# A transformer backbone in float32 halves on one core: three reorderings of the Vector engine's work, and wider pieces on GpSimd

## The chip, the cores and the metric

One core of one Trainium2 chip runs the whole program. The metric is the device time in microseconds (us) of one execution. The engines are TensorE (PE in the profile; PEld is its weight load), the Vector engine (DVE), the Scalar engine (ACT), GpSimd (POOL) and SyncE (SP), which issues the loads. "The profile" and "the trace" are one execution recorded by the hardware profiler.

## What is computed

Two layers over 512 latent tokens (`xl`) and 256 context tokens (`xc`) of width 1024. Each has a mixer (Fourier groups with neighbourhood attention, then differential attention) and a squared-ReLU MLP. DEPTH is 2, and layer 0 does the same for the context. The parts that the change touches, cut from the reference:

```python
def modulate(x, g, shift, scale):
    return rms_norm(x, g) * (1.0 + scale) + shift

def squared_relu_mlp(h, w_in, w_out):
    return jnp.square(jax.nn.relu(h @ w_in)) @ w_out

for i in range(DEPTH):
    ml = jnp.split((c_act @ w_mod[i] + b_mod[i])[:, None, :], 6, axis=-1)
    ...
    xl = xl + ml[5] * squared_relu_mlp(modulate(xl, norm_mlp_g[i], ml[3], ml[4]), w_mlp_in[i], w_mlp_out[i])
    ...
```

## The kernel before

**Numbers in two halves.** Each float32 operand is split in a high part (`w_hi`, `h_hi`, `hidh`) and a low part (`w_lo`, `h_lo`, `hidl`), and TensorE makes three products of the halves (lines 2090 to 2092, in `three`). Weights come in units of 128x1024. SyncE loads a unit into `raw` (four slots), the Scalar engine writes `w_hi` (`high_u`, `high_b`, `high_sum`), and GpSimd subtracts for `w_lo` (`low`, line 744), in as many pieces as its argument says; `lo_made` counts finished units. TensorE's `unit_done` frees the slot of `w_hi`, and `lo_made` the slot of `raw`.

**Every engine works through its own list in order.** The lists are written out by hand, and semaphores tie them together. So an instruction that waits holds up everything behind it on its engine.

**The first MLP** (`first_mlp` on each engine) has eight blocks of 512 hidden columns for 768 tokens. Block 0 is computed directly: the Scalar engine takes the relu of four tiles into `hidl_f`, the Vector engine squares each in place (`first_square`, line 1701), the Scalar engine rounds it into `hidh`, and the Vector engine makes `hidl` (`first_low`, line 1705). TensorE's `second(0, ...)` multiplies them with W_out: output tile 0 asks for `hq_made` (the four `hidl`) one after the other, and output tile 2 asks that tile 0 has been added to x by the Vector engine (`add_tile(0, 0)`, line 1662, counted by `x_added`). Blocks 1 to 7 use a seven-product scheme: GpSimd makes sums of the quadrants a11, a21, a12, a22 of the weights (`summed`, line 770), and the Vector engine makes the matching operands t1 to t4 of the activations once, in `difference` and `less` (lines 1689 to 1697): three instructions of 128x1536 for t1, and seven for t3, t2 and t4. `turn_high` and `turn_low` split them. The eighth block (`b == 7`) follows the sixth without a second product between them; I call that the last border. There GpSimd's `outer_sums` come behind `low(w, 4)`.

**The modulation vectors.** `mod_step(c, k)` on the Vector engine adds one of eight rows of chunk c (lines 1438 and 1441) from `mod_ring`, a ring of four buffers. Its last step also makes `acc_hi` and `acc_lo` (lines 1450, 1451). TensorE spreads the sum (`mod_mm`, lines 2131 and 2132), and `extract_late` takes the result out. SyncE's `load_mod` waits until the ring's buffer has been used, and all loads queued behind it wait too.

**The second MLP** (`mlp`) has four blocks of 16 units for 512 tokens, 24 matmuls of 512 columns a unit. Units 0 to 7 of a block give the hidden tiles (`hidden`, lines 1672, 1675, 1676, three Vector instructions), units 8 to 15 add to x. In its first block the Vector engine also does chunks 10 and 11. Before, chunk 10 stands at units 0 to 3, and `mod_mm(10, 6)` behind unit 5; chunk 11 stands at units 6, 7 and 8, and `mod_mm(11, 6)` behind unit 10. `MOD_LATE` says behind which unit's load SyncE issues which rows. The Scalar engine makes `w_hi` three units ahead, then the relu of the unit (line 1143), and its relu into one of two buffers waits for the Vector engine's first instruction of two tiles before. GpSimd's pieces are 1024 columns wide here, before and after.

Of the kernel before, what the change touches and what calls it, by code (L numbers as in the profile page):

```python
# [21 lines left out]
ALU = mybir.AluOpType  # L22
# [33 lines left out]

BLOCKS = 8
MOD_OF = {1: [0], 2: [1], 3: [2], 4: [3], 5: [4, 5], 6: [6], 7: [7]}
MOD_LATE = {1: (10, (4, 5)), 2: (10, (6, 7)), 4: (11, (0, 1)), 5: (11, (2, 3)), 7: (11, (4, 5)), 8: (11, (6, 7))}
M0, M1 = FIRST["mlp0"], FIRST["k1"]  # L60
RAWS = 64

# [5 lines left out]
def block_raw(b):  # L68
    return 8 * b if b < 7 else 52
# [60 lines left out]
def build(nc, t):  # L130

    ctx = ExitStack()
    with ctx:
# [602 lines left out]
        def _(pool):  # L736
            def low(u, pieces=1, b=None):

                pool.wait_ge(hi_made, u + 1 if b is None else u + 1 + 16 * b)
                r, s = raw_of(u), u % SLOTS  # L740
                src = w_sum if r is None else raw[:, r % SLOTS]
                for p in range(pieces):
                    sl = slice(p * (1024 // pieces), (p + 1) * (1024 // pieces))
                    ins = nc.gpsimd.tensor_tensor(w_lo[:, s, sl], src[:, sl], w_hi[:, s, sl].bitcast(F32),  # L744
                                                  op=ALU.subtract)
                ins.then_inc(lo_made, 1)
# [18 lines left out]
            def first_mlp():  # L765

                def summed(dst, a, b, op):
                    for p in range(4):
                        sl = slice(256 * p, 256 * p + 256)
                        ins = nc.gpsimd.tensor_tensor(dst[:, sl], a[:, sl], b[:, sl], op=op)  # L770
                    ins.then_inc(w_sums, 1)

                for w in range(4, 8):
                    low(M0 + w, 4)
                for b in range(1, BLOCKS):
                    w, r, n = M0 + block_first(b), M0 + block_raw(b), 4 * (b - 1)
                    a11, a21, a12, a22 = (raw[:, (r + j) % SLOTS] for j in range(4))

                    def raw_here(j):
                        pool.wait_ge(raw_in[(r + j) % SLOTS], 16 * ((r + j) // SLOTS + 1))  # L780

                    def outer_sums():
                        raw_here(1)
                        raw_here(3)
                        if b == 1:
                            pool.wait_ge(t_lo, 2)
                        else:
                            pool.wait_ge(lo_made, M0 + block_first(b - 1) + 4)
                        summed(w_sum, a21, a22, ALU.add)
                        raw_here(0)  # L790
                        pool.wait_ge(w_sums, n + 1)
                        summed(a21, a11, a21, ALU.subtract)

                    if b < 7:
                        outer_sums()
                    low(w, 4)
                    if b == 7:
                        outer_sums()
                    pool.wait_ge(w_sums, n + 2)
                    pool.wait_ge(lo_made, w + 1)  # L800
                    summed(a11, w_sum, a11, ALU.subtract)
                    low(w + 1, 4)
                    raw_here(2)
                    pool.wait_ge(w_sums, n + 3)
                    pool.wait_ge(lo_made, w + 2)
                    summed(w_sum, a12, a11, ALU.subtract)
                    for j in range(2, 11 if b < 6 else 7):
                        low(w + j, 4)
                for w in range(8):
                    low(M0 + LAST_W + w, 4)  # L810
                for u in range(AHEAD):
                    low(M1 + u, 4)

            def mlp():
                u0 = FIRST["mlp1"] + AHEAD + 1
# [610 lines left out]
        def _(dve):  # L1426
# [252 lines left out]
            def first_mlp():  # L1679
# [23 lines left out]
                def first_low(i):  # L1703
                    dve.wait_ge(hq_hi, i + 1)
                    tt(hidl[:, i], hidl_f[:, i], hidh[:, i].bitcast(F32), op=ALU.subtract).then_inc(hq_made, 1)  # L1705
# [3 lines left out]
                first_square(0)  # L1709
                first_square(1)  # L1710
                first_square(2)
                first_low(0)
                dve.wait_ge(tf_made, 1)
                difference(t3f[:], t4f[:], 1, H1, 0, H1)
                first_low(1)
                first_low(2)
                first_square(3)
                less(t2f[:], t1f[:], 1, 1, H1)
                first_low(3)
                less(t4f[:], t2f[:], 3, 1, H0)  # L1720

                def add_tile(b, m):
                    w = M0 + block_first(b) + (7 if b else 4) + m // 2
# [21 lines left out]
                for b in range(1, BLOCKS):  # L1745
                    c = MOD_OF[b][0]

                    def joined(side, p, q):
                        dve.wait_ge(unit_done, M0 + block_first(b) + p + 1)
                        dve.wait_ge(s_copied, 3 * (b - 1) + (3, 2, 1)[q])  # L1750
                        if q < 2 and b < 7:
                            dve.wait_ge(x_added, xa(0, min(b, 6) - 1, 7) + 1)
                        elif q < 2:
                            dve.wait_ge(hq_made, 4 * b)
                        tt(quarter_ps(b, q), part_ps(b, side), quarter(b, q)[2], op=ALU.add).then_inc(s_added, 1)

                    def low(q):
                        hi, lo, _ = quarter(b, q)
                        dve.wait_ge(hq_hi, 4 * b + q + 1)
                        tt(lo, quarter_ps(b, q), hi.bitcast(F32), op=ALU.subtract).then_inc(hq_made, 1)  # L1760

                    early = 4 if b < 5 else 6
                    steps(c, range(early))
                    joined(1, 3, 0)
                    steps(c, range(early, early + 1))
                    low(0)
                    joined(0, 4, 1)
                    steps(c, range(early + 1, early + 2))
                    low(1)
                    if b == 6:  # L1770
                        extract_late(c, 4)
                    joined(1, 5, 2)
                    low(2)
                    low(3)
                    if b < 5:
                        for m in range(8):
                            add_tile(b, m)
                            if m < 2:
                                steps(c, range(6 + m, 7 + m))
                            if m == 4:  # L1780
                                extract_late(c, 0)
                    elif b == 5:
                        add_tile(b, 0)
                        add_tile(b, 1)
                        extract_late(c, 0)
                        for m in range(2, 6):
                            steps(c + 1, range(2 * m - 4, 2 * m - 2))
                            add_tile(b, m)
                        add_tile(b, 6)
                        extract_late(c + 1, 0)  # L1790
                        add_tile(b, 7)
# [14 lines left out]
            def mlp():  # L1806
                u0 = FIRST["mlp1"]

                def blk(b, first, last):
                    for i in range(12 if last else 16):  # L1810
                        u = u0 + i
                        if i < 8:
                            hidden(b, i)
                        else:
                            if first and i in (8, 12):
                                dve.wait_ge(mod_done, PE_MODS + i // 4 + 9)
                            add_x(1, u + 16 * b + 1, u % 2, i - 8, 5, xa(1, b, i - 8))
                            if last and i > 8:
                                sum_squares(4, i - 9)
                        if first:  # L1820
                            if i == 5:
                                extract_late(10, 6)
                            elif i == 10:
                                extract_late(11, 6)
                            for k in (range(2 * i, 2 * i + 2) if i < 4 else {6: (0, 1, 2), 7: (3, 4, 5), 8: (6, 7)}.get(i, ())):
                                mod_step(10 if i < 4 else 11, k)

                blk(0, True, False)
                with st.loop(1, HID_BLOCKS - 1, 8) as b:
                    blk(b, False, False)  # L1830
                blk(HID_BLOCKS - 1, False, True)
# [253 lines left out]
        def _(pe):  # L2085
# [269 lines left out]
            def mlp(layer=1):  # L2355
# [3 lines left out]
                def blk(b, first, last):  # L2359
                    for i in range(12 if last else 16):  # L2360
# [21 lines left out]
                        elif i >= 8:  # L2382
                            unit(u + 16 * b, u % SLOTS, u % 2, *hid_t, chunks,
                                 (lambda k: pe.wait_ge(hid_made, ha(layer, b, k) + 1)) if i == 8 else None)
                        if first and i in (5, 10):
                            mod_mm(10 if i == 5 else 11, 6)

                blk(0, True, False)
                with pe.Fori(1, HID_BLOCKS - 1) as b:
# [571 lines left out]
```

## Time and profile before

| | us |
|---|---|
| median of 3 runs (1621.24 to 1622.34) | 1621.82 |
| the profiled execution: its time | 1622.5 |
| its span, first to last instruction | 1620.7 |
| TensorE busy in the span | 1578.3 (97%) |
| Vector / Scalar / GpSimd busy | 960.7 / 605.1 / 824.6 |

The profiled execution's time is 1.8 us more than its span, which lies around it. Times in the rows are us from the start of the span, an instruction's own duration in the lists of groups is in ns. A releaser after an arrow is what ended the idle time before an instruction.

### The profile page before, as it was taken

The page shows a single profiled execution, that of the slowest core. Times are in us where ns is not written, and L with a number is a line of the kernel's source. Part 1 is how long each engine was busy: PE and PEld are TensorE (multiplying, and loading weights), DVE is VectorE, ACT ScalarE, POOL GpSimd, SP SyncE. Part 2 cuts the span into 40 slices and gives each one's busy share as a digit, 9 for nine tenths or more (in the row PEclk, how much of TensorE's full clock was granted, in tenths as well). Part 3 has the DMA queues.
Part 4 walks back from the last instruction along what each step waited for, and adds up shares of the span by engine and source line. Part 5 has one row for each costly group of instructions (what it writes and reads, how often), then busy time and mean ns, then how long its engine had stood idle before and what let it go on. Part 6 is the DMA issues. An engine that isn't in the chain of part 4 may idle for free.

```text
span 1620.7 us, 23732 instructions
## 1 busy us (share of the span) xinstructions
PE 1578.3 (97%) x9272; PEld 1411.6 (87%) x9272; DVE 960.7 (59%) x1362; ACT 605.1 (37%) x1009; POOL 824.6 (51%) x778
## 2 busy tenths in 40 slices
PE   8999999997999999999899999999999799999998
PEld 5889988987999999999898888878889678888887
DVE  4697457258655555647466778059956755344264
ACT  4422466334243352441542411258844222222222
POOL 2422465337867868768852634245325444444441
PEclk9999999998999999999999999999999899999999
DMA  8473212212142242243352323110012342322221
GB/s 347 193 268 148 92 40 99 92 47 71 44 139 79 79 141 80 92 136 108 111 166 79 105 66 104 53 42 2 1 39 80 130 143 92 103 92 93 97 83 53
DMA packets 50346, 163.13 MB, mean 101 GB/s; under 512 B 6336, under 2 KB 8768, under 8 KB 46656
## 3 DMA queue, kind: packets, MB, share of 16 engines
q1 hardware_dynamic: 50240, 161.68, 29.3%
q8 instruction: 71, 1.16, 0.3%
q14 instruction: 35, 0.29, 0.1%
HBM read 158.78 MB, written 2.10 MB: 99 GB/s over the span
## 4 chain that ended last, share of the span: by engine, by line
PE 87%; DVE 6%; DMA 2%; issue 2%; POOL 2%; ACT 1%; SPq 0%; POOLq 0%; DVEq 0%; ACTq 0%
PE ps L2090 25%; PE ps L2091 24%; PE ps L2092 24%; PE ps L2729 3%; PE ps L2691 2%; PE ps L2718 1%; PE ps L2596 1%; PE ps L2584 1%; PE ps L2624 1%; PE ps L2408 1%; POOL w_lo L744 1%; DMA mod_late<-w_mod_dram 1%; DMA mod_big<-w_mod_dram 1%; DVE h L1564 1%; DVE mod_acc L1441 1%
## 5 line engine op out<-in xcount | busy, mean ns | idle before, releaser
L744 POOL TENSOR_TENSOR w_lo<-raw,w_hi 128x256 fp32r<-128x256 f32 (+1 forms) x443 | 552.5, 1273 | 598.0 <-ACT w_hi L951 405.7
L2090 PE MATMUL ps<-h,w_hi 128*128 128x512 f32 (+2 forms) x1016 | 357.9, 352 | 6.0 <-ACT tmp_a L1143 2.2
L2091 PE MATMUL ps<-h,w_lo 128*128 128x512 f32 (+2 forms) x1016 | 355.2, 350 | 0.0
L2092 PE MATMUL ps<-h,w_hi 128*128 128x512 f32 (+2 forms) x1016 | 354.7, 349 | 0.0
L2090 PEld LDWEIGHTS ps<-h,w_hi 128*128 128x128 f32 x1016 | 192.0, 189 | 31.0 <-issue 4.1
L2092 PEld LDWEIGHTS ps<-h,w_hi 128*128 128x128 f32 x1016 | 191.8, 189 | 17.3
L2091 PEld LDWEIGHTS ps<-h,w_lo 128*128 128x128 f32 x1016 | 192.0, 189 | 16.6
L1662 DVE SCALAR_TENSOR_TENSOR xl<-ps,mods,xl 128x384 f32<-128x384 f32 (+2 forms) x144 | 73.0, 540 | 218.1 <-PE ps L2092 216.7
L951 ACT ACTIVATE w_hi<-raw 128x1024 fp32r<-128x1024 f32 x120 | 126.4, 1054 | 116.5 <-PE ps L2092 110.8
L2090 PE MATMUL ps<-hidl,w_hi 128*128 128x384 f32 (+2 forms) x448 | 151.8, 339 | 10.5 <-DVE hidl L1705 9.4
L2091 PE MATMUL ps<-hidh,w_lo 128*128 128x384 f32 (+2 forms) x448 | 150.8, 337 | 0.0
L2092 PE MATMUL ps<-hidh,w_hi 128*128 128x384 f32 (+2 forms) x448 | 150.6, 336 | 0.0
L1441 DVE SCALAR_TENSOR_TENSOR mod_acc<-mod_ring,cact,mod_acc 128x512 f32<-128x512 f32 x112 | 106.9, 974 | 17.2 <-DVE mod_acc L1441 7.9
L958 ACT ACTIVATE w_hi<-raw 128x1024 fp32r<-128x1024 f32 x60 | 63.4, 1057 | 119.5 <-PE ps L2092 106.0
L2090 PE MATMUL ps<-hid_lo,w_hi 128*128 128x512 f32 (+1 forms) x288 | 106.0, 368 | 1.1 <-DVE hid_lo L1676 1.1
L2091 PE MATMUL ps<-hid_hi,w_lo 128*128 128x512 f32 (+1 forms) x288 | 105.3, 366 | 0.0
L2092 PE MATMUL ps<-hid_hi,w_hi 128*128 128x512 f32 (+1 forms) x288 | 105.3, 366 | 0.0
L2090 PEld LDWEIGHTS ps<-hidl,w_hi 128*128 128x128 f32 x448 | 84.8, 189 | 13.4 <-DVE hidl L1705 10.8
L2091 PEld LDWEIGHTS ps<-hidh,w_lo 128*128 128x128 f32 x448 | 84.9, 189 | 1.3 <-issue 0.2
L2092 PEld LDWEIGHTS ps<-hidh,w_hi 128*128 128x128 f32 x448 | 84.8, 189 | 0.6
L1672 DVE TENSOR_TENSOR tmp_b<-tmp_a 128x512 f32<-128x512 f32 x32 | 33.1, 1034 | 55.8 <-ACT tmp_a L1143 55.0
L1676 DVE TENSOR_TENSOR hid_lo<-tmp_b,hid_hi 128x512 fp32r<-128x512 f32 x32 | 63.7, 1989 | 1.1
(299 smaller groups left out, 3232.7 us busy)
## 6 DMA issues: line engine op xcount, KB each, us to landing
raw<-units_dram SPq DMA_DIRECT2D x187, 512.0 KB, 3.5
mod_ring<-w_mod_dram SPq DMA_DIRECT2D x96, 256.0 KB, 3.8
mod_big<-w_mod_dram SPq DMA_DIRECT2D x16, 1024.0 KB, 10.2
mod_late<-w_mod_dram SPq DMA_DIRECT2D x8, 1024.0 KB, 8.0
xl<-x_dram SPq DMA_DIRECT2D x2, 2048.0 KB, 8.3
bias<-bias_dram SPq DMA_DIRECT2D x8, 384.0 KB, 3.8
xc<-ctx_dram SPq DMA_DIRECT2D x2, 1024.0 KB, 10.4
out_dram<-out_t SPq DMA_DIRECT2D x16, 128.0 KB, 1.8
```

The lines of the kernel that those rows point to most:

```text
L744: ins = nc.gpsimd.tensor_tensor(w_lo[:, s, sl], src[:, sl], w_hi[:, s, sl].bitcast(F32), op=ALU.subtract)
L951: nc.scalar.activation(w_hi[:, u % SLOTS], raw[:, r % SLOTS], ACT.Copy).then_inc(hi_made, 1)
L958: nc.scalar.activation(w_hi[:, u % SLOTS], raw[:, r % SLOTS], ACT.Copy).then_inc(hi_made, 1)
L1441: ins = V.scalar_tensor_tensor(out=mod_acc[:, v], in0=w, scalar=cact[:, k, v:v + 1], in1=mod_acc[:, v], op0=ALU.mult, op1=ALU.add)
L1662: ins = V.scalar_tensor_tensor(out=x, in0=ps[:, 2 * par + bank, cols], scalar=gate(layer, m, v, i), in1=x, op0=ALU.mult, op1=ALU.add)
L1672: ins = tt(tmp_b[:, i % 2, 0:n], tmp_a[:, i % 2, 0:n], tmp_a[:, i % 2, 0:n], op=ALU.mult)
L1676: tt(hid_lo[:, i, 0:n], tmp_b[:, i % 2, 0:n], hid_hi[:, i, 0:n].bitcast(F32), op=ALU.subtract).then_inc(hid_made, 1)
L2090: mm(out, a[0], b[1], start=start, stop=False, skip_group_check=onto)
L2091: mm(out, a[1], b[0], start=False, stop=False, skip_group_check=onto)
L2092: return mm(out, a[0], b[0], start=False, stop=stop, skip_group_check=onto)
L2691: return mm(scores_ps(n)[:, TOK * i + keys.start:TOK * i + keys.stop], a[p][64 * i:64 * i + 64, tok], b[p][64 * i:64 * i + 64, keys], star ...
L2729: ins = mm(out_ps, v1[:, c, P * h:P * h + P], aturn[m % 2][:, c], start=c == 0, stop=c == NT - 1)
```

## The change

1. **First block**: the Vector engine makes `hidl` of all four tiles first, and t3, t2 and t4 come behind them.
2. **Last border**: the two `outer_sums` of block 7 move from GpSimd to the Vector engine, where they stand in block 6 behind the last step of the chunk and ahead of `low(1)`.
3. **Second MLP**: chunk 10 moves from units 0 to 3 to units 2 to 5, its `mod_mm` from behind unit 5 to behind unit 7; chunk 11 moves from units 6 to 8 to units 8 and 9, four rows at each, its `mod_mm` stays behind unit 10. `MOD_LATE` moves the loads of the rows to later units.
4. **Widths**: all of GpSimd's `low` and `summed` in `first_mlp` go from four pieces of 256 columns to two of 512.

```diff
-MOD_LATE = {1: (10, (4, 5)), 2: (10, (6, 7)), 4: (11, (0, 1)), 5: (11, (2, 3)), 7: (11, (4, 5)), 8: (11, (6, 7))}
+MOD_LATE = {6: (10, (4, 5)), 7: (10, (6, 7)), 8: (11, (0, 1)), 9: (11, (2, 3)), 11: (11, range(4, 8))}
...
                 def summed(dst, a, b, op):
-                    for p in range(4):
-                        sl = slice(256 * p, 256 * p + 256)
+                    for p in range(2):
+                        sl = slice(512 * p, 512 * p + 512)
...
                     if b < 7:
                         outer_sums()
-                    low(w, 4)
-                    if b == 7:
-                        outer_sums()
+                    low(w, 2)
...
                 first_square(2)
-                first_low(0)
+                for i in range(3):
+                    first_low(i)
+                first_square(3)
+                first_low(3)
                 dve.wait_ge(tf_made, 1)
                 difference(t3f[:], t4f[:], 1, H1, 0, H1)
-                first_low(1)
-                first_low(2)
-                first_square(3)
                 less(t2f[:], t1f[:], 1, 1, H1)
-                first_low(3)
                 less(t4f[:], t2f[:], 3, 1, H0)
+
+                def outer_sums(b):
+                    r, n = M0 + block_raw(b), 4 * (b - 1)
+                    a11, a21, _, a22 = (raw[:, (r + j) % SLOTS] for j in range(4))
+                    for j in (0, 1, 3):
+                        dve.wait_ge(raw_in[(r + j) % SLOTS], 16 * ((r + j) // SLOTS + 1))
+                    dve.wait_ge(lo_made, M0 + block_first(b - 1) + 4)
+                    tt(w_sum[:], a21, a22, op=ALU.add).then_inc(w_sums, 1)
+                    dve.wait_ge(w_sums, n + 1)
+                    tt(a21, a11, a21, op=ALU.subtract).then_inc(w_sums, 1)
...
                     steps(c, range(early + 1, early + 2))
+                    if b == 6:
+                        outer_sums(7)
                     low(1)
...
                         if first:
-                            if i == 5:
+                            if 2 <= i < 6:
+                                mod_step(10, 2 * i - 4)
+                                mod_step(10, 2 * i - 3)
+                            elif i == 7:
                                 extract_late(10, 6)
+                            elif i in (8, 9):
+                                for k in range(4 * i - 32, 4 * i - 28):
+                                    mod_step(11, k)
                             elif i == 10:
                                 extract_late(11, 6)
-                            for k in (range(2 * i, 2 * i + 2) if i < 4 else {6: (0, 1, 2), 7: (3, 4, 5), 8: (6, 7)}.get(i, ())):
-                                mod_step(10 if i < 4 else 11, k)
...
-                        if first and i in (5, 10):
-                            mod_mm(10 if i == 5 else 11, 6)
+                        if first and i in (7, 10):
+                            mod_mm(10 if i == 7 else 11, 6)
```

## Rows read from the trace of the kernel before

**Rows 1.** The waits of TensorE: us in total, times, longest.

```profile
PE ps L2090 <- DVE hidl L1705: 9.4, 2, 5.9
PE ps L2131 <- DVE acc_lo L1451: 6.8, 2, 6.5
PE ps L2090 <- POOL w_lo L744: 5.0, 2, 2.8
```

**Rows 2.** Stretches: busy us (instructions) of PE, PEld, DVE, ACT, POOL; PEclk, DMA share, GB/s.

```profile
392.00:416.00 24.00, 13.49 (x60) 11.86 (x59) 21.88 (x15) 8.48 (x9) 20.35 (x11) 0.72 0.24 78
416.00:780.00 364.00, 364.00 (x2094) 363.08 (x2094) 212.73 (x309) 127.34 (x145) 276.49 (x346) 1.00 0.32 104
780.00:808.00 28.00, 22.65 (x118) 21.64 (x117) 13.68 (x16) 13.70 (x17) 27.61 (x36) 0.94 0.15 48
...
1258.00:1310.00 52.00, 42.23 (x182) 34.20 (x182) 42.84 (x44) 13.29 (x17) 21.59 (x9) 0.90 0.41 134
```

**Rows 3.** Timeline of TensorE, first block: start, us, engine, line, operation, tiles, count.

```profile
407.40 0.69 PE L2090 MATMUL ps<-hidl,w_hi 128*128 128x384 f32 x1 [5.87 <-DVE hidl L1705]
...
408.21 0.52 PE L2092 MATMUL ps<-hidh,w_hi 128*128 128x384 f32 x1
...
415.65 0.33 PE L2090 MATMUL ps<-hidl,w_hi 128*128 128x384 f32 x1
```

**Rows 4.** Timeline of the Vector engine, around the first block.

```profile
378.52 1.76 DVE L1689 TENSOR_TENSOR t1f<-h 128x1536 f32<-128x1536 f32 x1 [2.16 <-POOL h L762]
...
390.65 2.29 DVE L1689 TENSOR_TENSOR t3f<-h 128x1536 f32<-128x1536 f32 x1
...
400.07 1.48 DVE L1701 TENSOR_TENSOR hidl_f<-hidl_f 128x768 f32<-128x768 f32 x1
...
413.77 0.88 DVE L1662 SCALAR_TENSOR_TENSOR xl<-ps,mods,xl 128x384 f32<-128x384 f32 x2 [2.01 <-PE ps L2092]
```

**Rows 5.** Timeline of GpSimd: the first block, block 6, the second MLP.

```profile
385.64 26.71 POOL L744 TENSOR_TENSOR w_lo<-raw,w_hi 128x256 fp32r<-128x256 f32 x16 [7.15 <-ACT w_hi L951]
...
771.92 2.81 POOL L744 TENSOR_TENSOR w_lo<-raw,w_hi 128x256 fp32r<-128x256 f32 x4 [1.35 <-ACT w_hi L951]
...
1302.59 2.40 POOL L744 TENSOR_TENSOR w_lo<-raw,w_hi 128x1024 fp32r<-128x1024 f32 x1 [3.03 <-ACT w_hi L958]
```

**Rows 6.** Timelines at the last border: Vector engine, GpSimd, TensorE.

```profile
781.62 1.11 DVE L1451 TENSOR_TENSOR acc_lo<-mod_acc,acc_hi 128x512 fp32r<-128x512 f32 x1
...
782.14 3.27 POOL L770 TENSOR_TENSOR w_sum<-raw 128x256 f32<-128x256 f32 x4
...
801.35 0.44 PE L2090 MATMUL ps<-t2l,w_hi 128*128 128x384 f32 x1 [2.84 <-POOL w_lo L744]
```

**Rows 7.** Timeline of the Vector engine, first units of the second MLP.

```profile
1267.83 0.69 DVE L1672 TENSOR_TENSOR tmp_b<-tmp_a 128x512 f32<-128x512 f32 x1
...
1269.62 0.75 DVE L1441 SCALAR_TENSOR_TENSOR mod_acc<-mod_ring,cact,mod_acc 128x512 f32<-128x512 f32 x1
1270.59 0.75 DVE L1441 SCALAR_TENSOR_TENSOR mod_acc<-mod_ring,cact,mod_acc 128x512 f32<-128x512 f32 x1 [0.21 <-DVE mod_acc L1441]
...
1284.95 2.71 DVE L1451 TENSOR_TENSOR acc_lo<-mod_acc,acc_hi 128x512 fp32r<-128x512 f32 x1
...
1302.65 2.88 DVE L1672 TENSOR_TENSOR tmp_b<-tmp_a 128x512 f32<-128x512 f32 x1 [0.21 <-DVE mod_acc L1441]
```

**Rows 8.** Timelines of SyncE and TensorE, first units of the second MLP.

```profile
1266.80 1.30 SPq L611 DMA_DIRECT2D mod_ring<-w_mod_dram  x2
1268.14 0.43 SPq L601 DMA_DIRECT2D raw<-units_dram  x1
...
1270.81 0.39 PE L2092 MATMUL ps<-h,w_hi 128*128 128x512 f32 x1
...
1271.49 0.39 PE L2092 MATMUL ps<-h,w_hi 128*128 128x512 f32 x1
...
1287.80 0.77 PE L2131 MATMUL ps<-acc_lo,ones 128*128 128x512 f32 x1 [6.46 <-DVE acc_lo L1451]
```

More of the change, by code:

```diff
@@ L773, in first_mlp @@
                 for w in range(4, 8):
-                    low(M0 + w, 4)
+                    low(M0 + w, 2)
                 for b in range(1, BLOCKS):
@@ L801, in first_mlp @@
                     summed(a11, w_sum, a11, ALU.subtract)
-                    low(w + 1, 4)
+                    low(w + 1, 2)
                     raw_here(2)
@@ L807, in first_mlp @@
                     for j in range(2, 11 if b < 6 else 7):
-                        low(w + j, 4)
+                        low(w + j, 2)
                 for w in range(8):
-                    low(M0 + LAST_W + w, 4)
+                    low(M0 + LAST_W + w, 2)
                 for u in range(AHEAD):
-                    low(M1 + u, 4)
+                    low(M1 + u, 2)
             def mlp():
```

## The prediction

> **What bounds the kernel now.** I read the share of busy time first: TensorE works in 97% of the span, so only its gaps can be won, and the clock it loses around them. The waits of TensorE name the gaps: the Vector engine's `hidl` with 9.4 us in two waits, its `acc_lo` with 6.8 in two, GpSimd's `w_lo` with 5.0 in two [rows 1]. The table by stage places them. From 416 to 780 TensorE is busy for 364.00 of 364 us at the full clock, though GpSimd works 276 us of it. The gaps are in the first block (13.5 busy of 24, clock 0.72), the last border (22.7 of 28, 0.94) and the second MLP's first units (42.2 of 52, 0.90) [rows 2]. The change aims at these three. A matmul of 384 columns takes 0.33 us at the full clock (2.4 GHz), 0.52 at half (1.2 GHz) [rows 3].
>
> **One price rules all three places: what a GpSimd piece costs a Vector instruction.** A 128x1536 subtraction takes 1.76 us alone and 2.29 beside GpSimd's 256-column pieces: +0.53 [rows 4]. A 128x512 one takes 0.69 alone and 2.88 beside a 1024-column piece: +2.2 [rows 7]. So the hold is 2.1 ns a column, and 512 columns cost about 1.07 per collision. Sixteen pieces of 256 take 26.7 us under the Vector engine's load, where alone four take 2.81 [rows 5]: the two engines go one for one. GpSimd's own time: 0.70 a piece at 256, 2.40 at 1024 [rows 5], by the line between them 1.26 at 512, so a unit takes 2.5 instead of 2.8.
>
> **First block.** Before, t3 stands among the `hidl`, and TensorE waits until 407.40 [rows 3]. After, GpSimd's four units are eight pieces, and each `hidl` step or square (1.48 less 0.53, of which 0.08 overlaps the next: 0.87 [rows 4]) pays 1.07: 1.94. Five of them from 389.7, when the first `hidl` starts as before (the instruction ahead of the 390.65 in [rows 4]) end at 399.4; the last `hidl` comes 8 us earlier and TensorE's first tile with it. But output tile 2 needs tile 0 added to x, and that stands on the Vector engine behind t3, t2, t4. Seven instructions at 1.68, one last collision and three own waits make 13.2: 412.6. Before, this chain ended at 413.77 less the 2.01 of idle time, 411.8 [rows 4]; it is not shortened, since all its work is still there and the pieces are wider. With 1.3 for the three adds TensorE starts tile 2 at 414.0, before at 415.65 [rows 3]: 1.65 earlier. It has then waited about 6 us, as before 407.40, and 3 us of work at half clock cost 1.5 again, now behind the start of tile 2. **Gain 0.2**; bounds +1.7 (no half clock behind the start) and -1.3 (twice the 1.5). A wait that moves, almost whole.
>
> **Last border.** Before, GpSimd starts the two sums at 782.14 [rows 6] and TensorE waits 5.0 for `w_lo` [rows 1], the last time until 801.35 [rows 6]. After, the Vector engine starts them when `acc_lo` ends, 782.7 [rows 6]. No row has 128x1024; between 0.69 for 512 and 1.76 for 1536 [rows 4, 7] lies 1.23. Two make 785.2. GpSimd then has four units' work to the `w_lo` of product 2, each 2.5: sum 787.7, `low` 790.2, sum 792.7, `low` 795.2. A product's 24 matmuls take 4.2 (2094 in 364 us [rows 2]). From 801.35 back through both waits (5.0) and a slow restart (0.3), TensorE would reach product 2 at 796.1, product 1 at 791.9 and product 0 at 787.75, so none waits. That is 5.2 less idle time; the granted clock of 0.94 over 28 us [rows 2] is 3.4 us at half, worth 1.7. Beside it: `low(1)`, the extraction (three short instructions) and the join of the third quarter come 2.5 later. The first product of block 7 needs the extraction: done at 787.7, just in time. One collision of 1.07 there would cost 1.0; I take 0, since the two long ones read PSUM. The Scalar engine's list (nine instructions of 0.8, three of 1.06 behind the third quarter) ends its copy at 796, even with product 2. SyncE's loads wait for `w_lo`, which comes earlier; none is moved. **Gain 6.9**, bounds 5.0 and 7.2.
>
> **Second MLP.** What the old order did: SyncE's unit load stood behind rows whose buffers the Vector engine freed late (1266.80, then the unit at 1268.14) [rows 8], and `acc_lo` ended at 1287.66 [rows 7], so TensorE waited 6.46 [rows 8]. In all it waited 2.2, 6.5 and 1.1, and 3.2 more went to the half clock. Without them it reaches the end of unit 7 at 1271.88 plus three units: 24 matmuls at 0.227 (1270.81 to 1271.49 is three [rows 8]) are 5.46, so 1288.2. Is `acc_lo` there? The first tile's relu is there at 1260.2, just before unit 3 starts (1271.88 less two units, 1261.0). From then the Vector engine owes six hidden tiles at 1.8 (1267.83 to 1269.62), eight steps at 0.96 [rows 7], and the split with 1.1: 19.6. And now that loads 6 and 7 are early, GpSimd's units follow one another without a pause: units 4 to 11 fall in that time, eight collisions. Seven or eight at 2.1 make 15 to 17. The engine never catches up: `acc_lo` at 1295.1. **TensorE waits 6.9 us here**, once and later, with 1.6 for the clock. Then chunk 11: its rows 4 to 7 stand behind the add of unit 9. Add 0.75, four steps 3.8, split 1.1, two collisions 4.2 (units 13 and 14) are 9.9, and TensorE needs it after unit 10, 5.46 later: a **new wait of 4.5** and 1.4 for the clock. From 1295.1: the spread 0.9, three units 16.4, the clock 1.6, that wait: the spread of chunk 11 at 1318.2, before at 1318.3, and the clock after it on top. With some tenths for the restarts this stage is **2.0 later** than before. Bounds: 3.5 later (three collisions at chunk 11), 1.0 earlier (one fewer at each place).
>
> The Trainium skill (SBUF — State Buffer, "Who interferes with whom") says that GpSimd and a Vector instruction with two SBUF inputs share a port pair that is held exclusively for the full instruction. By that rule a collision costs the whole 2.40 us and not 2.1 to 2.2, and the sum would be 1619.2. The trace speaks for the smaller price, with 2.71 for an `acc_lo` that takes 0.69 itself [rows 7].
>
> **GpSimd's widths elsewhere.** In blocks 1 to 6 fewer, longer holds: 0.53 times four or 1.07 times two for a unit, the same sum. TensorE's full 364 us [rows 2] cover it; I cost it at nothing. If that cover went, a block could lose a few tenths.
>
> **Sum.** 0.2 + 6.9 - 2.0 = 5.1 off. The profiled execution's 1622.5 (span 1620.7 and 1.8 around it) would become 1617.4; it stands 0.7 above the median of 1621.8, which becomes **1616.7**. About 0.2%, 3.2 us, is what a measurement of this kernel can tell from no change.
>
> **Rivals.**
> - *The second MLP does as the order suggests.* The Vector engine catches up in units 2 to 5, in spite of the collisions. For it: 3.7 us of own work to 5.46 a unit. Against: with one collision a unit it is 5.8. It gives 10 to 13 more: 1604 to 1607. 0.12.
> - *The gain is eaten.* The border's sums come late (the extraction misses product 0, the Scalar copy misses product 2: 2 us and the clock's 1.7), or chunk 11 meets a third collision. 1619 to 1622. 0.15.
> - *Each collision costs the whole piece.* A Vector instruction behind a 1024-column piece starts only when its 2.40 us are over [rows 5], 0.25 more than I take; ten collisions make 2.5: 1619.2. (This is the rule of the Trainium skill's SBUF page.) For: one for one in [rows 5]. Against: 2.71 for `acc_lo` [rows 7] with its own 0.69 leaves 2.0. 0.05.
> - *Slower: wide pieces stall the steady blocks.* In blocks 1 to 6 the Vector engine's steps stand ahead of a join for which TensorE waits; a hold of 1.07 instead of 0.53 could push each join. It decides from 1.4 us a block (six make 8.4, over the 5.1 and the 3.2). Against: not one wait in 364 us [rows 2], and joins read PSUM. At 2 us a block: 1629. 0.03.
> - The forecast itself: 0.65.
>
> Its own range is 1614.5 to 1618.6; a tenth of the chance of its case lies above 1618.6. Faster: 0.60 and 0.12, so 0.72; same 0.25; slower 0.03. For 8 in 10 the range reaches over the eaten gain and towards the first rival: 1611.0 to 1620.5.
>
> **What would show it.** In the profile after: TensorE's waits for `hidl` under 6 us, and a new one of about 6 before output tile 2, released by the Vector engine's add; no wait for `w_lo` between 780 and 808; `acc_lo` still the longest, twice, near 7 and near 4.5 us; GpSimd 512-column pieces of 1.29 us alone. I am wrong if the wait for chunk 10 is gone, if the steady blocks show gaps, or if tile 2 starts without waiting.

## The result, and the profile after

The changed kernel takes 1630.05 us (median of 5 runs, 1628.9 to 1631.07), the kernel before 1621.75 beside it: the ratio is 1.0055, with a 95% interval of 1.0043 to 1.0066. It is slower by 8 to 9 us where I forecast 5 faster. The profiled span is 1629.1, 8.4 more than before.

The waits of TensorE in the changed kernel (us in total, times, longest), to be read against [rows 1]; `three` is now at lines 2103 to 2105 and `mod_mm` at 2144:

```profile
PE ps L2144 <- DVE acc_lo L1449: 12.8, 3, 7.5
PE ps L2103 <- DVE xc L1660: 11.7, 6, 6.2
PE ps L2144 <- DVE xc L1660: 3.1, 1, 3.1
PE ps L2103 <- DVE hidl L1703: 3.1, 1, 3.1
```

GpSimd's `w_lo` is gone from the top, and the Vector engine's add to x (`xc`, line 1660), which was in no wait before, stands there with 11.7 us in six and 3.1 in one. The stretches answer to [rows 2] (the last one is shifted by 4 us and 16 us longer, so that both long waits of the changed kernel lie in it; it holds 237 matmuls where the one of before holds 182):

```profile
392.00:416.00 24.00, 13.77 (x59) 12.99 (x60) 22.95 (x17) 9.43 (x9) 7.19 (x5) 0.83 0.19 66
416.00:780.00 364.00, 355.34 (x2020) 352.31 (x2019) 232.03 (x302) 120.85 (x137) 236.39 (x169) 0.99 0.29 96
780.00:808.00 28.00, 27.59 (x157) 26.79 (x156) 15.01 (x18) 16.31 (x20) 18.41 (x15) 1.00 0.32 108
1262.00:1330.00 68.00, 55.52 (x237) 45.49 (x236) 54.27 (x53) 15.32 (x19) 27.84 (x12) 0.87 0.40 132
```

From 416 to 780 TensorE is busy for 355.3 us and no longer for 364.0. That stretch was the firm ground of my argument. The border is repaired (27.6 of 28 where 22.7 was; it now lies 11.5 us later, and the stretch from 791.5 to 819.5 is busy for the same 27.59), and the second MLP's first units have 12.5 us of gaps. TensorE's timeline names the longest ones (start, duration, and in brackets the wait and its releaser):

```profile
412.56 0.66 PE L2103 MATMUL ps<-hidl,w_hi 128*128 128x384 f32 x1 [6.16 <-DVE xc L1660]
...
487.37 0.41 PE L2103 MATMUL ps<-hidl,w_hi 128*128 128x384 f32 x1 [1.32 <-DVE xc L1660]
...
762.58 0.65 PE L2144 MATMUL ps<-acc_lo,ones 128*128 128x512 f32 x1 [3.13 <-DVE xc L1660]
...
1300.08 0.77 PE L2144 MATMUL ps<-acc_lo,ones 128*128 128x512 f32 x1 [7.48 <-DVE acc_lo L1449]
...
1324.64 0.76 PE L2144 MATMUL ps<-acc_lo,ones 128*128 128x512 f32 x1 [5.00 <-DVE acc_lo L1449]
```

I also compared when like matmuls start in the two traces, the n-th with the n-th. A plus is time lost against the profile of before (us; one execution each; e1 and the others are told below):

| | up to the first block | first block | blocks 1 to 4 | blocks 5, 6 and the border | second MLP |
|---|---|---|---|---|---|
| changed kernel | -1.5 | +1.0 | +6.2 | -1.0 | +4.1 |
| e1, 256 columns, all three reorderings | -1.3 | +0.8 | 0.0 | -6.1 | +4.0 |
| e2, 512 columns alone | -0.5 | +2.7 | +8.9 | +1.5 | +0.7 |
| e3, the border alone | -1.5 | +1.4 | 0.0 | -6.1 | -3.5 |
| e4, the second MLP alone | -3.0 | +1.0 | 0.0 | -1.6 | +3.7 |
| e5, the first block alone | -1.6 | -0.2 | 0.0 | +0.1 | -0.1 |

The first column is work that the change doesn't touch: it differs by up to 3 us from one execution to the next, so a stage is read here to about 1.5 us and a kernel by its timed runs (e4 shows -1.6 at a border that it leaves as it was). The changed kernel loses 6.2 in blocks 1 to 4; its -1.0 behind them is 5.7 lost in block 5 and 6.7 won at the border, read at the matmul that starts at 770 us in the profile of before. TensorE's gap of 1.32 us stands once in each of blocks 1 to 4, the one of 3.13 in block 5.

### The profile page after: what moved, and what is told of

Same layout as the page of the kernel before. It is cut to its first block, busy times and chain, and to the rows that moved or that the text cites. A ratio compares the mean times of both kernels' runs of the same rounds, so it can differ in the third digit from the quotient of the medians.

```text
span 1629.1 us, 23506 instructions
## 1 busy us (share of the span) xinstructions
PE 1579.2 (97%) x9272; PEld 1412.8 (87%) x9272; DVE 997.2 (61%) x1364; ACT 604.9 (37%) x1009; POOL 762.6 (47%) x550
## 4 chain that ended last, share of the span: by engine, by line
PE 82%; DVE 11%; issue 3%; DMA 1%; ACT 1%; SPq 0%; POOL 0%; DVEq 0%; POOLq 0%; ACTq 0%
PE ps L2103 23%; PE ps L2104 23%; PE ps L2105 23%; DVE mod_acc L1439 3%; PE ps L2742 3%; PE ps L2704 2%; PE ps L2731 1%; PE ps L2609 1%; PE ps L2597 1%; PE ps L2637 1%; PE ps L2421 1%; DVE acc_hi L1448 1%; DVE xl L1660 1%; DMA mod_big<-w_mod_dram 1%; DVE early_acc L1461 1%
## 5 line engine op out<-in xcount | busy, mean ns | idle before, releaser
L744 POOL TENSOR_TENSOR w_lo<-raw,w_hi 128x512 fp32r<-128x512 f32 (+2 forms) x303 | 515.0, 1717 | 630.9 <-ACT w_hi L949 425.8
L2103 PE MATMUL ps<-hidl,w_hi 128*128 128x384 f32 (+2 forms) x448 | 153.5, 343 | 15.8 <-DVE xc L1660 11.7
L1439 DVE SCALAR_TENSOR_TENSOR mod_acc<-mod_ring,cact,mod_acc 128x512 f32<-128x512 f32 x112 | 133.7, 1214 | 13.1 <-DVE mod_acc L1439 8.8
L2103 PEld LDWEIGHTS ps<-hid_lo,w_hi 128*128 128x128 f32 x288 | 55.5, 193 | 10.4 <-DVE hid_lo L1674 1.2
```

What stands on the lines that cost most here:

```text
L1439: ins = V.scalar_tensor_tensor(out=mod_acc[:, v], in0=w, scalar=cact[:, k, v:v + 1], in1=mod_acc[:, v], op0=ALU.mult, op1=ALU.add)
L2103: mm(out, a[0], b[1], start=start, stop=False, skip_group_check=onto)
```

## The experiments

**Which part costs what.** Four kernels ran beside the kernel before. The first two divide the change in widths and order.

```diff
 # e1: the changed kernel, and in GpSimd's first_mlp
-                    for p in range(2):
-                        sl = slice(512 * p, 512 * p + 512)
+                    for p in range(4):
+                        sl = slice(256 * p, 256 * p + 256)
...
-                    low(w, 2)
+                    low(w, 4)
```

> The changed kernel with GpSimd's pieces back at 256 columns: the three reorderings alone. Theory (a Vector instruction pays one hold for each collision, and the hold grows with the width of the piece): the gaps of TensorE between 416 and 780 us (1.32 us in each of blocks 1 to 4, 3.1 us in block 5) vanish, some 12 us with the clock, and the time is about 1618.5. Rival (the gaps come from the reorderings, by the phase in which the first block leaves the engines): the gaps stay and the time is about 1630.

Measured: 1620.44 us, ratio 0.9995 (0.9986 to 1.0004). Its stretches from 416 to 780 and from 780 to 808:

```profile
416.00:780.00 364.00, 364.00 (x2089) 363.09 (x2089) 210.14 (x307) 126.81 (x145) 277.29 (x347) 1.00 0.32 104
780.00:808.00 28.00, 27.19 (x153) 26.17 (x152) 16.09 (x19) 16.23 (x20) 24.81 (x32) 1.00 0.23 76
```

The steady stretch is full again, and at the border 27.2 us of 28 are busy. The reorderings together are worth nothing that can be measured (by the table, -6.1 at the border and +4.0 in the second MLP), and the loss is the widths'.

```diff
 # e2: the kernel before, and in GpSimd's first_mlp
-                    for p in range(4):
-                        sl = slice(256 * p, 256 * p + 256)
+                    for p in range(2):
+                        sl = slice(512 * p, 512 * p + 512)
...
-                    low(w, 4)
+                    low(w, 2)
```

> The kernel before with GpSimd's pieces at 512 columns and nothing else. Theory: the gaps of blocks 1 to 5 appear here too (+12 us), the first block loses about 1.5, the last border gains about 3: about 1632. Rival (the gaps need the reorderings): 1617 to 1622.

Measured: 1632.85, ratio 1.0069 (1.0056 to 1.0083). The stretch from 416 to 780:

```profile
416.00:780.00 364.00, 354.24 (x2009) 351.25 (x2008) 234.21 (x304) 119.65 (x136) 232.41 (x166) 0.99 0.30 95
```

Ten us of gaps with no reordering in the kernel. The rival of this pair, that the order brings the gaps, is out.

```diff
 # e3: the kernel before, with the Vector engine's outer_sums(b) of the change, and
-                    if b == 7:
-                        outer_sums()
...
                     steps(c, range(early + 1, early + 2))
+                    if b == 6:
+                        outer_sums(7)
```

> The kernel before with block 7's two outer sums moved to the Vector engine and nothing else. As predicted: TensorE's waits for w_lo between 780 and 808 us go, and the slow clock behind them; about 6.2 us faster, 1615.6. Rival (the Vector engine's later extraction gives it back): within 2 us of the kernel before.

Measured: 1616.42, ratio 0.997 (0.9958 to 0.9981), 4.6 us under the 1621.02 of the kernel before on the same chip. Between like matmuls the border is 6.1 shorter, and no wait for `w_lo` is left there. The whole gained less than the stage, and the record shows why: 1.6 of the 6.1 are the clock that the profiled execution of before lost behind its second wait. In e9 (below), which leaves the border as it was, the same two waits stand there (5.0 us in all), and the clock doesn't fall:

```profile
780.00:808.00 28.00, 22.64 (x127) 21.62 (x126) 11.79 (x15) 12.84 (x15) 27.61 (x37) 1.00 0.20 65
```

127 matmuls start where [rows 2] has 118 in the same busy time at 0.94. Without those 1.6 the border is worth 4.5, and the timed runs say 4.6.

```diff
 # e4: the kernel before, MOD_LATE as in the change, and
-                            if i == 5:
+                            if 2 <= i < 6:
+                                mod_step(10, 2 * i - 4)
+                                mod_step(10, 2 * i - 3)
+                            elif i == 7:
                                 extract_late(10, 6)
+                            elif i in (8, 9):
+                                for k in range(4 * i - 32, 4 * i - 28):
+                                    mod_step(11, k)
...
-                        if first and i in (5, 10):
-                            mod_mm(10 if i == 5 else 11, 6)
+                        if first and i in (7, 10):
+                            mod_mm(10 if i == 7 else 11, 6)
```

> The kernel before with the second MLP's new order of chunks 10 and 11 and nothing else. Theory (four GpSimd pieces in a row put the Vector engine 6 us behind, and it cannot catch up): TensorE waits near 7 us for chunk 10 and near 5 us for chunk 11, about 4 us slower, 1625.8. Rival (the backlog comes from what the first MLP left, not from the order itself): faster than before.

Measured: 1623.74, ratio 1.0019 (1.001 to 1.0029), 2.7 us slower, with the first MLP untouched. I had expected 1625.8; the waits of 7.48 and 5.00 us are both there. The new order of the second MLP, its loads included, does it by itself.

**The first block alone.**

```diff
 # e5: the kernel before, and
-                first_low(0)
+                for i in range(3):
+                    first_low(i)
+                first_square(3)
+                first_low(3)
...
                 difference(t3f[:], t4f[:], 1, H1, 0, H1)
-                first_low(1)
-                first_low(2)
-                first_square(3)
                 less(t2f[:], t1f[:], 1, 1, H1)
-                first_low(3)
```

> The kernel before with the first block's new order alone, pieces at 256 columns. As predicted: the wait for hidl shrinks by some 8 us and comes back whole as a wait of TensorE for the Vector engine's add before output tile 2; within 1.5 us of the kernel before. Rival (the earlier first tile is worth its 8 to 10 us): 1611 to 1613.

Measured: 1621.52, ratio 1.0004 (0.9994 to 1.0013). The wait of TensorE that takes the place of those for `hidl`:

```profile
PE ps L2089 <- DVE xc L1662: 9.3, 1, 9.3
```

The first tile is done long before, and TensorE then waits 9.3 us for the add of output tile 0, which stands behind t3, t2 and t4.

**What a wide piece costs the steady blocks.** The changed kernel's Vector engine in block 1, between the adds of output tiles 1 and 2: two steps, the cast to `acc_hi`, `acc_lo`, and the add for which TensorE waits.

```profile
479.67 2.44 DVE L1439 SCALAR_TENSOR_TENSOR mod_acc<-mod_ring,cact,mod_acc 128x512 f32<-128x512 f32 x2
482.25 1.56 DVE L1448 CAST acc_hi<-mod_acc 128x1024 fp32r<-128x1024 f32 x1
483.85 2.19 DVE L1449 TENSOR_TENSOR acc_lo<-mod_acc,acc_hi 128x1024 fp32r<-128x1024 f32 x1
485.96 0.86 DVE L1660 SCALAR_TENSOR_TENSOR xl<-ps,mods,xl 128x384 f32<-128x384 f32 x2
```

GpSimd beside it, at the sums:

```profile
480.14 3.12 POOL L770 TENSOR_TENSOR w_sum<-raw 128x512 f32<-128x512 f32 x2 [3.79 <-issue]
483.40 3.77 POOL L770 TENSOR_TENSOR raw<-raw 128x512 f32<-128x512 f32 x2
```

The same four instructions in the kernel before take from 480.15 to 484.78, 4.6 us and not 6.3:

```profile
480.15 1.89 DVE L1441 SCALAR_TENSOR_TENSOR mod_acc<-mod_ring,cact,mod_acc 128x512 f32<-128x512 f32 x2
482.19 1.00 DVE L1450 CAST acc_hi<-mod_acc 128x1024 fp32r<-128x1024 f32 x1
483.22 1.64 DVE L1451 TENSOR_TENSOR acc_lo<-mod_acc,acc_hi 128x1024 fp32r<-128x1024 f32 x1
484.78 0.86 DVE L1662 SCALAR_TENSOR_TENSOR xl<-ps,mods,xl 128x384 f32<-128x384 f32 x2
```

The pair of steps, the cast and `acc_lo` grow by 0.55, 0.56 and 0.55: one wider hold each. (The first step of the pair begins before GpSimd's first piece and takes 0.74 in both kernels; the second one takes 1.23 and 1.78.) Three instructions meet one piece each, whatever its width; the pieces are longer, and there are no fewer collisions. The dose was doubled once more:

```diff
 # e8: the kernel before, with one piece
-                    for p in range(4):
-                        sl = slice(256 * p, 256 * p + 256)
+                    for p in range(1):
+                        sl = slice(1024 * p, 1024 * p + 1024)
...
-                    low(w, 4)
+                    low(w, 1)
```

> The kernel before with GpSimd's pieces in the first MLP as one of 1024 columns. Theory (price per Vector instruction, not per column of GpSimd's work): the hold doubles again to 2.1 us, so the gaps of blocks 1 to 4 grow from 1.3 to some 4 to 6 us each and block 5's from 3 to some 8; about 1650. Rival, as I predicted (the same GpSimd columns hold the Vector engine for the same sum, whatever the width): no slower than with 512 columns, 1633 or less, since GpSimd's own time falls once more.

Measured: 1659.72, ratio 1.0241 (1.0224 to 1.0258), 10 us more than I expected. The same place in block 1:

```profile
480.49 3.55 DVE L1441 SCALAR_TENSOR_TENSOR mod_acc<-mod_ring,cact,mod_acc 128x512 f32<-128x512 f32 x2
484.18 2.67 DVE L1450 CAST acc_hi<-mod_acc 128x1024 fp32r<-128x1024 f32 x1
486.88 3.25 DVE L1451 TENSOR_TENSOR acc_lo<-mod_acc,acc_hi 128x1024 fp32r<-128x1024 f32 x1
490.06 0.86 DVE L1662 SCALAR_TENSOR_TENSOR xl<-ps,mods,xl 128x384 f32<-128x384 f32 x2
```

480.49 to 490.06 is 9.6 us: 4.6, 6.3 and 9.6 for pieces of 256, 512 and 1024 columns, and the last step again is 3.3, three times 1.1. TensorE's gap in blocks 1 to 4 is 4.59 us each, as expected; between like matmuls a block loses 7.1 on average, and the rest goes with the granted clock, 0.97 over the stretch:

```profile
416.00:780.00 364.00, 343.72 (x1915) 340.79 (x1913) 236.74 (x280) 116.34 (x132) 207.16 (x81) 0.97 0.28 91
```

GpSimd is busy for 207 us there, for 236 with 512 columns and 276 with 256 [rows 2]: its own work gets cheaper and the kernel slower (a part of the fall is that the slower kernels have less work in the stretch, 1915 matmuls for 2094). The sum that I had held constant doubles with the width.

Which pieces? The changed kernel with only line 770's sums narrow:

```diff
 # e10: the changed kernel, and in summed alone
-                    for p in range(2):
-                        sl = slice(512 * p, 512 * p + 512)
+                    for p in range(4):
+                        sl = slice(256 * p, 256 * p + 256)
```

> The changed kernel with only the sums of weight quadrants (line 770) back at 256 columns, all w_lo pieces still 512 wide. Theory: the Vector engine's four instructions at output tile 1 of blocks 1 to 4 collide with sums and with nothing else, so the gap of 1.3 us in blocks 1 to 4 goes, while block 5's gap, whose eight steps meet both kinds, shrinks but stays; about 1623.5. Rival (it is the total width, or the w_lo pieces): the four gaps stay, 1628 or more.

Measured: 1618.21, ratio 0.9983 (0.9974 to 0.9992), some 12 us less than the changed kernel. The Vector engine and GpSimd in block 1:

```profile
480.21 1.89 DVE L1439 SCALAR_TENSOR_TENSOR mod_acc<-mod_ring,cact,mod_acc 128x512 f32<-128x512 f32 x2
482.25 1.00 DVE L1448 CAST acc_hi<-mod_acc 128x1024 fp32r<-128x1024 f32 x1
483.28 1.64 DVE L1449 TENSOR_TENSOR acc_lo<-mod_acc,acc_hi 128x1024 fp32r<-128x1024 f32 x1
484.85 0.86 DVE L1660 SCALAR_TENSOR_TENSOR xl<-ps,mods,xl 128x384 f32<-128x384 f32 x2
```

```profile
474.35 2.53 POOL L744 TENSOR_TENSOR w_lo<-raw,w_hi 128x512 fp32r<-128x512 f32 x2 [0.78 <-ACT w_hi L949]
480.60 4.92 POOL L770 TENSOR_TENSOR w_sum<-raw 128x256 f32<-128x256 f32 x4 [3.71 <-issue]
...
488.44 2.54 POOL L744 TENSOR_TENSOR w_lo<-raw,w_hi 128x512 fp32r<-128x512 f32 x2
```

The Vector engine's group is back at 4.6 us. And block 5's gap went too, which I had not expected (I had said 1623.5): it has no gap left over 0.25 us. With the sums narrow, the `w_lo` pieces of 512 columns cost almost nothing. In block 5 they still meet two of the chunk's steps (1.52 and 1.49 us), the cast (1.29) and `acc_lo` (1.66), but that group has slack enough now: TensorE loses 0.3 us there.

A step could also be moved instead:

```diff
 # e6: the changed kernel, and in blocks 1 to 4
-                            if m < 2:
-                                steps(c, range(6 + m, 7 + m))
+                            if m in (0, 2):
+                                steps(c, range(6 + m // 2, 7 + m // 2))
```

> The changed kernel, 512-column pieces kept, with the chunk's last step (and its split in two halves) moved in blocks 1 to 4 from behind output tile 1 to behind output tile 2. Theory (four Vector instructions between the adds of tiles 1 and 2 each pay one hold, and the add of tile 2 comes 1.3 us after TensorE wants it): the gap of 1.32 us in blocks 1 to 4 vanishes, the gap in block 5 stays; about 6 us faster than the changed kernel, 1624. Rival (a share of GpSimd's or the loads' lateness makes the gap): the gaps stay, or others of the same size appear at later tiles.

Measured: 1630.39, ratio 1.0058 (1.0042 to 1.0075): nothing won. The gap has moved to the spread ahead of output tile 5, which waits for the add of tile 3, now behind the group:

```profile
491.75 0.50 PE L2144 MATMUL ps<-acc_lo,ones 128*128 128x512 f32 x1 [1.30 <-DVE xc L1660]
```

My expectation failed, as the rival's second half said. The group of four starts two output tiles' adds later and ends at 490.5, and the next add that TensorE needs is as close behind it. The run doesn't tell a collision from another cause; it shows that the list has no slack of 1.3 us at either place.

**The second MLP, with narrow pieces.** There `mlp` makes GpSimd's pieces 1024 wide in every kernel so far. Its first units in the changed kernel, Vector engine and GpSimd:

```profile
1265.79 2.78 DVE L1674 TENSOR_TENSOR hid_lo<-tmp_b,hid_hi 128x512 fp32r<-128x512 f32 x1
1268.50 2.87 DVE L1670 TENSOR_TENSOR tmp_b<-tmp_a 128x512 f32<-128x512 f32 x1
1271.40 2.52 DVE L1673 CAST hid_hi<-tmp_b 128x512 fp32r<-128x512 f32 x1
1273.96 2.76 DVE L1674 TENSOR_TENSOR hid_lo<-tmp_b,hid_hi 128x512 fp32r<-128x512 f32 x1
```

```profile
1265.60 10.57 POOL L744 TENSOR_TENSOR w_lo<-raw,w_hi 128x1024 fp32r<-128x1024 f32 x4 [3.27 <-ACT w_hi L956]
...
1320.87 2.61 POOL L744 TENSOR_TENSOR w_lo<-raw,w_hi 128x1024 fp32r<-128x1024 f32 x1 [3.03 <-ACT w_hi L956]
```

Four units of GpSimd in a row (10.57 us), and four Vector instructions that take 0.69, 0.69, 0.43 and 0.69 us alone and 2.5 to 2.9 here. That is the backlog of the prediction. If it is the collisions, narrow pieces remove it. (The loop that is edited makes 48 of the 64 units; the last twelve keep one piece.)

```diff
 # e7: e4, and in GpSimd's mlp
-                        low(u0 + i, 1, b)
+                        low(u0 + i, 4, b)
 # e9: the kernel before, and there
-                        low(u0 + i, 1, b)
+                        low(u0 + i, 8, b)
```

> The second MLP's new order alone, as in the run before (1623.7), with GpSimd's pieces in the second MLP at 256 columns instead of 1024. Theory: the start of the first block costs the Vector engine four collisions of 0.53 instead of 2.1, it catches up, chunk 10's wait falls from 7.5 us to under 2 and chunk 11's from 5 to about 1; 9 to 11 us faster than that run, about 1613.5. Rival (the backlog is the Vector engine's own work): less than 3 us faster.

Measured: 1610.56, ratio 0.9936 (0.992 to 0.9953), 13 us under e4 where I had expected 9 to 11. The waits of TensorE from 1200 to 1350:

```profile
PE ps L2135 <- DVE acc_lo L1451: 2.8, 2, 1.6
PE ps L2094 <- DVE hid_lo L1676: 0.7, 1, 0.7
```

> The kernel before, its own order of chunks 10 and 11, with GpSimd's pieces in the second MLP at 128 columns instead of 1024. Theory: each collision costs 0.27 us; chunk 10's split is ready when TensorE asks, nearly all of the 9.8 us of waits and the slow clock behind them go: about 10 us faster, 1611. Rival (GpSimd's units, 3.6 us instead of 2.4, come too late for TensorE): gaps for w_lo appear and half or more of that is lost.

Measured: 1608.74, ratio 0.9928 (0.9911 to 0.9945). The waits of TensorE in the same stretch, and the Vector engine's `hid_lo` of tiles 0 and 1 and its `acc_lo`:

```profile
PE ps L2090 <- POOL w_lo L744: 2.3, 3, 1.0
```

```profile
1257.70 0.83 DVE L1676 TENSOR_TENSOR hid_lo<-tmp_b,hid_hi 128x512 fp32r<-128x512 f32 x1
...
1261.62 0.83 DVE L1676 TENSOR_TENSOR hid_lo<-tmp_b,hid_hi 128x512 fp32r<-128x512 f32 x1
...
1273.34 0.83 DVE L1451 TENSOR_TENSOR acc_lo<-mod_acc,acc_hi 128x512 fp32r<-128x512 f32 x1
```

`acc_lo` takes 0.83 where it took 2.71 [rows 7], and TensorE doesn't wait for it at all. What is left is GpSimd: three waits, 2.3 us in all, for a unit that takes eight pieces. The rival of e7 is out, and that of e9 for the larger part. The two runs don't compare the two orders, since they differ in the width as well; the old order with four pieces was not run.

**The best version.** Two stages that don't touch each other, then a third thing:

```diff
 # e11: e3 and e9 together;  e12: e11, and
                 for w in range(4, 8):
-                    low(M0 + w, 4)
+                    low(M0 + w, 8)
```

> The kernel before with two things: block 7's outer sums on the Vector engine (-4.6 us alone) and GpSimd's pieces in the second MLP at 128 columns (-11.7 us alone). The two lie in different stages, so they add: about 1604.5. If they share a cause or a slack, less than 14 us is won.

Measured: 1605.2, ratio 0.9901 (0.9886 to 0.9916), 15.4 us under the kernel before where the two alone make 16.3. They add.

> The kernel of the run before this one, with GpSimd's four w_lo units of the first block in pieces of 128 columns. By the price per collision (0.27 instead of 0.53) the Vector engine's chain of the first block ends about 2 us earlier: some 2 us faster, about 1602.5. Rival: GpSimd's last unit of the block comes too late, and nothing is won.

Measured: 1603.11, ratio 0.9889 (0.9874 to 0.9904). Its page's busy times and the first of TensorE's waits for `hidl` and `w_lo`:

```profile
PE 1571.6 (98%) x9272; PEld 1407.3 (88%) x9272; DVE 920.8 (57%) x1364; ACT 604.9 (38%) x1009; POOL 895.3 (56%) x1122
```

```profile
PE ps L2100 <- DVE hidl L1703: 7.4, 2, 4.8
...
PE ps L2100 <- POOL w_lo L744: 2.3, 3, 1.0
```

It is 2.1 us under e11, as expected, but with four runs of each the two intervals overlap; what speaks for the 2 us is that the waits for `hidl` fall from 9.4 to 7.4 us. GpSimd is busy for 895 us where it was for 825, the Vector engine for 921 and not 961, and this kernel has the lowest median of all.

## Why the prediction was wrong

- **The step that failed**: "GpSimd's widths elsewhere", where I wrote "0.53 times four or 1.07 times two for a unit, the same sum", and costed it at nothing. Where the Vector engine's instructions stand closely and GpSimd has work, their number sets the collisions, not that of GpSimd's pieces. Three of them meet three pieces at 256, at 512 and at 1024. I had the right rule two paragraphs above ("the two engines go one for one") and used it in the first block and in the second MLP, not here. The sum lacks 10 to 12 us by it: e1 and e10 are 9.6 and 11.8 us under the changed kernel, and e2 is 11.8 over the kernel before. By the matmuls it is 6.2 in blocks 1 to 4 and 5.7 in block 5, 11.9 of the 13.5 us between forecast and profile (1617.4 and 1630.9). Of the rest 2.1 are the second MLP and 1.2 the first block, while 1.5 came off ahead of all that was changed, which is luck.
- **"TensorE's full 364 us cover it"** was the second half of that error. A full TensorE says that nobody waited, not by how much. The group in block 1 got 1.66 us longer (6.29 for 4.63) and the gap behind it is 1.32, so the cover was 0.34 us. The rival "wide pieces stall the steady blocks" has this mechanism, and its turning point of 1.4 us a block; I gave it 0.03, and "if the steady blocks show gaps" was my own sign of being wrong. Blocks 1 to 4 lose 1.6 each (6.2 in all), block 5 loses 5.7. Its place was not quite right: not a join (the Vector engine's add of two partial products), but the adds of the output tiles.
- **First block**: right within what one profile tells. Predicted a gain of 0.2 and a wait of about 6 us for the add before tile 2; the wait is 6.16 in the changed kernel, 9.3 with 256 columns, and e5's interval holds no change. Tile 2 starts at 412.56 where it started at 415.65 [rows 3], of which 1.5 was there before the block: 1.6 earlier, where I said 1.65. Behind it the changed kernel is 1.0 later by the table, inside my bounds; but e3 and e4, which leave this block as it was, are 1.0 to 1.4 later as well.
- **Last border**: right in mechanism, over in size: 6.1 to 6.7 between like matmuls for 6.9, but 4.6 by the timed runs of e3, under my bound of 5.0. The term that doesn't hold in every execution is the clock's 1.7: it was lost in the profile that I read, and e9's has the same waits at a clock of 1.00.
- **Second MLP**: right in mechanism, under in size. I forecast waits of 6.9 and 4.5 us, they are 7.48 and 5.00, and 2.0 us later; the profile of the changed kernel is 4.1 later, e4 2.7 by its median. My sum had a slip: 1295.1 with 0.9, 16.4, 1.6 and 4.5 is 1318.5 and not 1318.2, so the forecast should have read 2.3. The two waits are 1.1 over. What the clock adds, e10 shows. It has the same two waits (7.47 and 4.99) and the same busy times of the other engines in the 68 us that answer to the changed kernel's, but it is granted 0.92 there and not 0.87:

```profile
1251.20:1319.20 68.00, 55.53 (x244) 45.66 (x243) 54.27 (x53) 15.32 (x19) 27.84 (x12) 0.92 0.41 132
```

  Between like matmuls e10's stage is 2.5 later and not 4.1. So the granted clock of the execution makes the same instructions and waits cost 1.6 us more or less. The rival "does as the order suggests" got 0.12 and is out in this form; e7 shows that it needed narrow pieces as well.
- **The full hold**: the Trainium skill (SBUF — State Buffer, "Who interferes with whom") has the pair held for the whole instruction. The four collisions above cost 2.78 less 0.69, 2.87 less 0.69, 2.52 less 0.43 and 2.76 less 0.69: 2.07 to 2.18 us, where a 1024-column piece alone takes 2.40. That is the smaller price that I took, and ten collisions at 2.1 don't make the 2.5 us more that the Trainium skill's rule would. What is missing is the same at every width (last section), so it isn't a share of the hold; whether it is a fixed part of each instruction that runs beside the other's, the runs don't say. That the loser stands still, and isn't slowed in proportion, fits them: the instruction of 0.43 us pays 2.09 and the first one of 0.69 pays 2.09 as well.

**Left open.** In the execution of e3 that was profiled the second MLP is 3.5 us shorter than in the profile of before, with the same instructions there (TensorE's longest wait for `acc_lo` is 2.4 us and not 6.5); its time of 1613.6 is short against e3's median of 1616.4 as well. What decides between two courses of the same instructions, and between two clocks behind the same wait, I did not try; nor did I try where the first column's 0.5 to 3 us come from.

## What to carry to other kernels

Where two engines take turns at something, price a wider piece by the instructions of the *other* engine that it meets, one hold each, and not by the total of the work; make the pieces narrow where the other engine's list is what someone waits for, and wide only where it is slack. A stretch in which the bound engine is 100% busy has a slack that must be read, from the end of the work to the start of its use, before anything in it is called covered. And when a chain is reordered, ask which later consumer stands behind the part that moved back.

## What the runs showed of the hardware

The price of one collision can be read at four widths from one shape, the subtraction of 128x512 that makes `hid_lo` or `acc_lo` and takes 0.69 us alone. Beside pieces of 128 and 1024 columns it takes 0.83 and 2.76 (rows above); beside 256 (e7) and 512 (the changed kernel) it takes

```profile
1259.69 1.11 DVE L1676 TENSOR_TENSOR hid_lo<-tmp_b,hid_hi 128x512 fp32r<-128x512 f32 x1
...
759.72 1.63 DVE L1449 TENSOR_TENSOR acc_lo<-mod_acc,acc_hi 128x512 fp32r<-128x512 f32 x1
```

So it pays 0.14, 0.42, 0.94 and 2.07 us. GpSimd's pieces take 0.46 (e9), 0.74 (before), 1.29 (the changed kernel) and 2.40 [rows 5] alone: the price is the piece's own time less 0.32 to 0.35 at each width. My 2.1 ns a column from zero is right for wide pieces and too dear for narrow ones, 0.27 for 128 columns. Other instructions pay somewhat more or less: the subtraction in [rows 4] 0.53 at 256 columns, a step of the chunk that takes 0.75 alone 0.18 or 0.48. Instructions that read PSUM pay nothing: the two adds to `xl` take 0.86 to 0.88 in the rows of block 1 at each of the three widths. GpSimd's unit takes 2.40 us in one piece [rows 5] and 3.39 in eight (e9, alone), and eight were still the better bargain by 11.7 us.
